# Linear attention in a two-block language-model kernel: keys moved into the exponent, a new order of the score levels, and the read-out and norm by halves

## The reference

```python
def step(state, inp):
    qb, kb, vb, gb = inp
    cum = jnp.cumsum(gb, axis=2)
    o_inter = jnp.einsum('bhtk,bhkv->bhtv', qb * jnp.exp(cum), state)
    rel = cum[:, :, :, None, :] - cum[:, :, None, :, :]
    decay = jnp.exp(jnp.where(causal, rel, -jnp.inf))
    scores = jnp.einsum('bhtk,bhsk,bhtsk->bhts', qb, kb, decay)
    o_intra = jnp.einsum('bhts,bhsv->bhtv', scores, vb)
...
forget = lower_bound + (1.0 - lower_bound) * jax.nn.sigmoid(f.astype(F32))
logf = jnp.log(forget)
k = 1.0 - forget
...
o = rms_norm(o, out_norm) * jax.nn.silu(heads(g.astype(F32)))
return o.reshape(b_, s_, D_MODEL).astype(x.dtype) @ w_out
```

## Time and profile before

| | |
|---|---|
| median of 3 runs | 1805.54 us (1802.91 to 1806.9) |
| the profiled execution | 1802.63 us, span 1800.2 us |
| PE / DVE / ACT / POOL busy | 1717.4 / 1275.4 / 995.2 / 188.5 us |
| linear attention, W0 to the first `down` | 1174.1 to 1274.1 us of the span |

### The profile page before, as it was taken

One profiled execution on the slowest core, in us unless ns is written; L12 is line 12 of the kernel. 1 busy time (PEld: TensorE's weight loads), 2 busy tenths in 40 slices (PEclk: granted clock), 3 DMA queues, 4 the chain that ended last, 5 costly groups with the idle time before them and its releaser, 6 DMA issues.

```text
span 1800.2 us, 35518 instructions
## 1 busy us (share of the span) xinstructions
PE 1717.4 (95%) x11627; PEld 1576.6 (88%) x11627; DVE 1275.4 (71%) x2201; ACT 995.2 (55%) x1476; POOL 188.5 (10%) x108
## 2 busy tenths in 40 slices
PE   7999999999999999999999999999899998799998
PEld 6998879999989999978888887978699998689997
DVE  5866664589997777767777777798666665566665
ACT  6653445675756666644545555654455455564554
POOL 0022300234220000000000000075000000100000
PEclk9999999999999999999999999999899999899999
DMA  5542255577765555567787776442255554045553
GB/s 186 164 151 72 81 178 198 164 210 216 207 214 175 175 175 175 178 217 243 238 280 238 243 239 225 155 138 94 82 188 188 186 185 136 34 141 187 185 185 107
DMA packets 114412, 316.67 MB, mean 176 GB/s; under 512 B 12752, under 2 KB 45904, under 8 KB 113840
## 3 DMA queue, kind: packets, MB, share of 16 engines
q1 hardware_dynamic: 113504, 311.88, 53.7%
q0 software_dynamic: 848, 4.00, 0.6%
HBM read 296.95 MB, written 18.87 MB: 175 GB/s over the span
## 4 chain that ended last, share of the span: by engine, by line
PE 83%; DVE 11%; ACT 3%; issue 2%; DMA 0%; POOL 0%; ACTq 0%; DVEq 0%; SPq 0%; POOLq 0%
PE bank L259 14%; PE bank L260 14%; PE bank L261 14%; PE bank L301 10%; PE bank L302 10%; PE bank L303 10%; PE bank L1288 3%; DVE wlo L243 2%; DVE arena L1860 1%; PE bank L1691 1%; PE bank L996 1%; ACT whi L235 1%; DVE arena L1876 1%; DVE arena L1408 1%; DVE h L452 1%
## 5 line engine op out<-in xcount | busy, mean ns | idle before, releaser
L243 DVE TENSOR_TENSOR wlo<-raw,whi 128x1024 fp32r<-128x1024 f32 x502 | 637.5, 1273 | 218.6 <-ACT whi L235 206.5
L259 PE MATMUL bank<-xhi,whi 128*128 128x256 f32 (+1 forms) x2424 | 707.0, 292 | 14.6 <-DVE wlo L243 7.8
L261 PE MATMUL bank<-xhi,wlo 128*128 128x256 f32 (+1 forms) x2424 | 690.3, 285 | 0.0
L260 PE MATMUL bank<-xlo,whi 128*128 128x256 f32 (+1 forms) x2424 | 690.1, 285 | 0.0
L235 ACT ACTIVATE whi<-raw 128x1024 fp32r<-128x1024 f32 x524 | 550.9, 1053 | 110.3 <-PE bank L303 58.6
L259 PEld LDWEIGHTS bank<-xhi,whi 128*128 128x128 f32 x2424 | 466.8, 193 | 23.5 <-issue 13.4
L260 PEld LDWEIGHTS bank<-xlo,whi 128*128 128x128 f32 x2424 | 467.5, 193 | 1.7
L261 PEld LDWEIGHTS bank<-xhi,wlo 128*128 128x128 f32 x2424 | 466.5, 192 | 0.0
L301 PE MATMUL bank<-whi,yhi 128*128 128x512 f32 x816 | 320.9, 393 | 8.8 <-DVE ylo L585 4.4
L302 PE MATMUL bank<-wlo,yhi 128*128 128x512 f32 x816 | 319.9, 392 | 0.0
L303 PE MATMUL bank<-whi,ylo 128*128 128x512 f32 x816 | 319.3, 391 | 0.0
(11 more groups left out here) (288 smaller groups left out, 1570.6 us busy)
## 6 DMA issues: line engine op xcount, KB each, us to landing
raw<-in_stream SPq DMA_DIRECT2D x524, 512.0 KB, 3.5
act_spill<-h SPq DMA_DIRECT2D x128, 128.0 KB, 3.0
h<-act_spill SPq DMA_DIRECT2D x128, 128.0 KB, 3.3
h<-in_x SPq DMA_DIRECT2D x1, 1024.0 KB, 5.1
arena<-in_keys POOLq DMA_DIRECT2D x1, 1024.0 KB, 6.5
h_spill<-h SPq DMA_DIRECT2D x1, 1024.0 KB, 7.7
arena<-h_spill POOLq DMA_DIRECT2D x1, 1024.0 KB, 5.9
arena<-in_g_final POOLq DMA_DIRECT2D x1, 512.0 KB, 8.0
```

The source lines that it names most:

```text
L243: nc.vector.tensor_tensor(wlo[:, q * 1024:(q + 1) * 1024], raw[:, q * 1024:(q + 1) * 1024], whi[:, q * 1024:(q + 1) * 1024].bitcast(F32), ...
L259: nc.tensor.matmul(bank[b][:, 0:T], whi[:, w], xhi[:, x], start=k == 0, stop=False)
L260: nc.tensor.matmul(bank[b][:, 0:T], whi[:, w], xlo[:, x], start=False, stop=False)
L261: last = nc.tensor.matmul(bank[b][:, 0:T], wlo[:, w], xhi[:, x], start=False, stop=k == KT - 1)
```

## The change

Keys go into the exponent: ACT takes the logarithm of the keys (`CKN`, one more 128x2048 activation after the forget gates' logarithm), POOL subtracts it from `CUM` head by head (eight 128x256 instructions), and the key side of a level is then one exponential. `k_side` is gone from DVE and POOL; `differences` becomes two 128x1024 instructions instead of one of 128x2048. The order of the levels on PE is 8, 0, 1, ..., 7, and which slabs follow each level stands in `AFTER`: two slabs and one in turn. Level matmuls wait for the banks of the level before one by one, and W8 for the copied value banks one by one. The read-out, squares, sums, roots and gating go by halves (heads 0 to 3, then 4 to 7); the norm and the gate are one DVE instruction per head and token tile; the norm's gain is a per-partition scalar `ONC` (one more transpose, of `ONR`), applied when the result is split, straight from PSUM, so that the copy to SBUF and POOL's multiplication are gone. The second half's eight transposes stand between D2 and D3.

```diff
+        LEVEL_ORDER = (8, 0, 1, 2, 3, 4, 5, 6, 7)
+        AFTER = {8: (2,), 0: (3, 4), 1: (5,), 2: (6, 7), 3: (8,), 4: (9, 10), 5: (11,), 6: (12, 13), 7: (14, 15)}
...
+            pe.wait_ge(s("onr_in"), 16)
+            nc.tensor.transpose(bank[7][:, 0:P], ONR, ident[:, :]).then_inc(s("onr_tr"), 1)
             pe.wait_ge(up_evac, U_HG + 16 + 2)
...
+            wide(0)
+            wide(1)
+            pe.wait_ge(s("q_silu"), 1)
+            pe.wait_ge(s("onc"), 1)
+            for x in LEVEL_ORDER:
+                level(x)
+                for k in AFTER[x]:
+                    wide(k)
             pe.wait_ge(s("level_out"), 4 * 9)
...
+            read_out(0)
+            read_out(1)
             pe.wait_ge(s("g_out"), 4)
...
+            turned_out(0)
+            down(pe, N_HGO, D_HGO, 0, 0, 4, first=True)
+            down(pe, N_HGO + 1, D_HGO + 1, 0, 0, 4)
+            down(pe, N_HGO + 2, D_HGO + 2, 0, 0, 4)
+            pe.wait_ge(y_lo, D_HGO + 4)
+            turned_out(1)
...
+                if j == 2:
+                    nc.scalar.activation(CKN, KK, ACT.Ln, bias=LEAST).then_inc(s("logk"), 1)
...
+            level_exp(0)
+            split(0)
+            level_exp(1)
+            for k in (1, 2, 3):
+                split(k)
+            for x in range(2, 8):
+                level_exp(x)
+                for k in AFTER[x - 2]:
+                    split(k + 1)
...
+            split(0)
+            q_side(0)
+            split(1)
+            split(2)
             take(8)
...
+            q_side(1)
+            split(3)
+            for x in range(8):
+                take(x)
+                for k in AFTER[x]:
+                    if k < 15:
+                        split(k + 1)
+                if x + 2 < 8:
+                    q_side(x + 2)
...
+            sums(0)
+            sums(1)
+            gated(0)
+            gated(1)
+            y(0)
...
+            for hd in range(HG_H):
+                q = slice(hd * SEQ, (hd + 1) * SEQ)
+                pool.wait_ge(s("cum"), hd + 1)
+                nc.gpsimd.tensor_tensor(CKN[:, q], CUM[:, q], CKN[:, q], ALU.subtract).then_inc(s("ckn"), 1)
+            pool.wait_ge(s("ckn"), 8)
```

More of the change, by code:

```diff
@@ L1701, in pe_hgrn @@
-            level(8)
-            pe.wait_ge(s("level_out"), 4 * 9)
[L1703 to L1713, removed]
@@ L1714, in pe_hgrn @@
-            pe.wait_ge(s("g_out"), 4)
[L1715 to L1722, removed]
@@ L1723, in pe_hgrn, with read_out @@
-            down_pe(pe, N_HGO, D_HGO, 8)
+            wide(0)
[6 more added lines that the diff above has]
+                    wide(k)
+            pe.wait_ge(s("level_out"), 4 * 9)
+            def read_out(half):
+                for tt in range(TT):
+                    for hd in range(4 * half, 4 * half + 4):
+                        o = bank[4 + 2 * tt + half][:, (hd % 4) * P:(hd % 4 + 1) * P]
+                        v = lambda c: VT[:, c * D + hd * P:c * D + (hd + 1) * P]
+                        if tt == 0:
+                            last = nc.tensor.matmul(o, PP[:, hd * SEQ:hd * SEQ + P], v(0), start=True, stop=True)
+                        else:
+                            nc.tensor.matmul(o, CR[:, hd * P:(hd + 1) * P], v(0), start=True, stop=False)
+                            last = nc.tensor.matmul(o, PP[:, hd * SEQ + P:(hd + 1) * SEQ], v(1),
+                                                    start=False, stop=True)
+                    last.then_inc(s("o_mm"), 1)
@@ new lines, in turned_out @@
+            def turned_out(half):
+                pe.wait_ge(s("o_gated"), 8 * half + 8)
+                for j in range(4):
+                    for tt in range(TT):
+                        c = tt * D + (4 * half + j) * P
+                        last = nc.tensor.transpose(bank[j][:, half * SEQ + tt * P:half * SEQ + (tt + 1) * P],
+                                                   OO[:, c:c + P], ident[:, :])
+                    last.then_inc(s("o_tr"), 1)
+            read_out(0)
+            read_out(1)
@@ L1725, in act_hgrn, with halves @@
+        def halves(ap, half):
+            return ap.rearrange("p (t a h) -> p a t h", t=TT, a=2)[:, half]
         def act_hgrn(act, chain):
@@ new lines, in act_hgrn @@
+            split(0)
[6 more added lines that the diff above has]
+                    split(k + 1)
+                    if k == 7:
+                        act.wait_ge(slabs_done, N_HG + 16 + 8 + RING)
+                        for b in range(4):
+                            nc.scalar.activation(VT[:, b * 512:(b + 1) * 512], bank[b][:, :], ACT.Copy)\
+                                .then_inc(s("v_out"), 1)
@@ L1772, in act_hgrn @@
+            for k in (12, 13, 14):
+                split(k + 1)
+            nc.scalar.activation(tiny[:, 29:30], V("one"), ACT.Silu)
             act.wait_ge(slabs_done, N_HG + 32 + RING)
-            for b in O_ORDER:
+            for b in (0, 2, 1, 3):
                 nc.scalar.activation(GS[:, b * 512:(b + 1) * 512], bank[b][:, :], ACT.Silu).then_inc(s("g_out"), 1)
-            nc.scalar.activation(tiny[:, 28:29], V("one"), ACT.Sqrt)
[L1777 to L1780, removed]
@@ L1797, in dve_hgrn @@
+            squares(0)
+            nc.scalar.activation(tiny[:, 28:29], V("one"), ACT.Sqrt)
+            squares(1)
+            roots(0)
+            roots(1)
+            y(0)
+            for j in range(7):
+                y(j + 1)
+                split_hi(act, N_HGO + j + AHEAD, 0, 0, 4)
         def dve_hgrn(dve, chain):
@@ new lines, in gated @@
+            def gated(half):
+                dve.wait_ge(s("o_rt"), half + 1)
+                chain.link(nc.vector.reciprocal(halves(ORS, half), halves(ORT, half)))
+                for tt in range(TT):
+                    b = 2 * tt + half
+                    if half == 0:
+                        dve.wait_ge(s("g_out"), tt + 1)
+                    else:
+                        dve.wait_ge(s("g_out"), 4)
+                    for hd in range(4):
+                        q = slice(b * 512 + hd * P, b * 512 + (hd + 1) * P)
+                        nc.vector.scalar_tensor_tensor(out=OO[:, q], in0=bank[4 + b][:, hd * P:(hd + 1) * P],
+                                                       scalar=ORS[:, 4 * b + hd:4 * b + hd + 1], in1=GS[:, q],
+                                                       op0=ALU.mult, op1=ALU.mult).then_inc(s("o_gated"), 1)
@@ L1921, in pool_hgrn @@
+            y(0)
+            for j in range(7):
+                y(j + 1)
+                split_lo(dve, N_HGO + j + AHEAD, 0, 0, 4)
         def pool_hgrn(pool, chain):
```

180 lines of the change are left out of this document (84 added, 96 removed).

## The result

The changed kernel takes 1813.31 us (median of 5 runs, 1811.25 to 1813.89), the kernel before beside it 1804.92 us (5 runs, 1802.68 to 1806.9): ratio 1.0041, 95% interval 1.0027 to 1.0056. It is slower by 8.4 us; 1809.2 was forecast. The profiled execution took 1811.25 us, with a span of 1809.6.

A forecast was written before the change was run, and what follows sets the result against it. PE, busy 95% of the span, was taken as the bound, so only its waits could be gained. Levels +5.7 us and tail -2.0 gave +3.7, or 1809.2 us on the median; range 1806.5 to 1813.5.

The forecast's parts named there:

- The start: From the last `up` slab to level 0: PE waits 5.3 us, in two or three pieces; level 0 starts at 1191.6.
- rival A: Start of the levels: scans pass POOL, so level 0 starts 4.2 us sooner; 1805.0 us, within 0.2%; chance 0.20.
- 22.6 us in all: DVE and POOL's shared budget until difference 1 is done: scans 4.8, splits 4.6, subtractions 5.6, halves 7.6 us.
- The next chain: From level 0's end to level 2: 17.0 us against 12.2 us of cover, so PE waits 4.8 us.
- The rest of the levels: From level 2 on: PE has 50.3 us of work plus small waits, ending W15 at 1263.8; levels cost 5.7 us more.
- I add 1.4 us in all, and 1.7 for one fall of the clock: From level 2 on: allowance for chains of 11.5 to 14 us against 12.2, and for slower clock behind longer waits.
- The tail: From the read-out to D0: 12.8 us, 3.1 sooner; 1.1 us of transposes return between D2 and D3; gain 2.0.
- The rest of the kernel is the same: Outside the changed linear attention: no difference in time was charged.
- B: Levels: cheap start and chains that fit, level 2 at 1202.7; 5.7 us faster, 1799.8 us; chance 0.20.
- C: POOL's difference halves cost 2.37 us each, adding 12 us; 1817.5 us; chance 0.12.
- in ACT's waits: Before the scans: the keys' logarithm, 1.9 us on ACT, hides while ACT waits for `up` slabs.
- the first to ask goes first: Throughout the levels: POOL and DVE's SBUF instructions share one time budget, served in order of asking.

The follow-up runs named there:

- spaced: Changed kernel with slabs respread, two after nearly every level and none behind level 7: median 1808.42 us, ratio to before 1.0023.
- third_buffer: Changed kernel with three QK buffers instead of two, so a difference waits for an earlier level's matmuls: 1800.11 us, one execution.
- tail_only: Kernel before with only the new read-out, norm, gating and result split; old keys and level order: median 1804.56 us, ratio 0.9999.
- no_sub: Changed kernel without POOL's eight subtractions of the keys' logarithm, keys left out of all levels but level 8: median 1804.01 us, ratio 0.9997.
- levels_only: Changed kernel with the old tail: only keys in the exponent, new level order and places, banks freed singly: median 1813.19 us, ratio 1.0040.
- sub_on_dve: Changed kernel with the keys' logarithm subtracted by DVE in two 128x1024 instructions behind the first split after the scans: 1804.29 us, one execution.
- three_edits: Changed kernel with three QK buffers, the keys' logarithm subtracted on DVE, and level 8's take directly behind slab 0's split: median 1796.46 us, ratio 0.9945.
- replanned: Changed kernel with the subtraction on DVE and a new written order on all three engines, two buffers: median 1796.91 us, ratio 0.9952.

## Why the prediction was nearly right

The sign, the places and the mechanisms hold; the sizes less so. Forecast for the stage +3.7 us, measured +4.6, and that it came so near is in part luck, since errors of 2.8 and 1.4 us stand against one of 6.1. The time lies 0.2 us inside the upper end of my range (1806.5 to 1813.5); the difference of 8.4 us lies outside my +1 to +8.

*The start, forecast 5.3 us of waits.* Measured 1.13 + 0.37 + 1.40 = 2.9. Scans do take turns with POOL's subtractions (7.16 us), so rival A's premise fell; the last `up` slab waited 1.13 us. But difference 1 ended at 1185.41 us, 60.8 after the stage began, where my sum gave 1185.1 - 1122.05 = 63.0. The term "22.6 us in all" was too large: from 1165.76 to 1185.41 it took 19.7. Scans and subtractions together took 9.2 us, so a subtraction added about 0.55 us where I took 0.7, and the rest of splits and halves took 10.5 for 12.2, in part because the first split (from 1172.84) ran beside the last subtractions. Level 2 began 85.6 us into the stage, 2.8 sooner than the sum says (1210.4 - 1122.05 = 88.4).

*The next chain, forecast 17.0 us and a wait of 4.8.* Measured from level 0's end (1193.6) 16.6 and 4.79. `spaced` shows the cover to be the cause, `third_buffer` the chain.

*The rest of the levels, the step that failed.* The term that was mis-sized is "I add 1.4 us in all, and 1.7 for one fall of the clock": the waits are 1.93 + 2.20 = 4.1 us, and two levels were slowed, by 2.7 and 1.7 us. I had taken the later chains as 11.5 to 14 us against 12.2 of cover and charged almost nothing for it. The longer wait also cost more clock than the one that I copied from the earlier trace rows. From level 2 to the read-out PE took 58.1 us, where I had 53.4. In `third_buffer`, where nothing waits on this stretch, it took 48.9 us (1209.54 to 1258.42), where my sum has 50.3. So waits and clock cost 9.2 us for my 3.1, and 1.4 of these 6.1 us were hidden by slabs and levels priced too high, 2.8 by the overestimate at the start. (The 3.62 us that I read as a level in the earlier trace rows are rows of 30 matmuls; a level there has 32, as the row of 5.46 us says, and not 16.)

*The tail, forecast 12.8 us to D0 and -2.0 in all.* 12.2 us to D0. In all -3.7 + 0.8 = -2.9 us in the changed kernel, and -2.7 in `tail_only`.

*"The rest of the kernel is the same."* True of the code, not of the time: 2.3 us in the windowed attention, in both profiles, at a lower granted clock. If the unprofiled executions behave alike, which no run shows, that makes with the stage's 4.6 us 6.9 of the 8.4 between the medians; the remaining 1.5 lie within the interval (4.9 to 10.1 us), and the starts alone scatter by more. The distance of 4.1 us from my 1809.2 would then be 0.9 from the stage and 2.3 from there; what is left is not more than this scatter.

*The rivals.* A and B needed a cheap start. `no_sub` gave one, and levels 2, 4 and 5 still waited: B's chains don't fit in this order. C's price was not met: alone a half takes 1.93 us, key half or not; the means over the levels, 2.46 us for a query half and 2.93 for a key half, hold the waits for DVE. That the keys' logarithm hides "in ACT's waits" was not wholly so: the scans began 41.1 us into the stage, as in `no_sub` and `levels_only`, which have it too, and 40.5 before and in `tail_only`, which don't.

The Trainium skill (SBUF — State Buffer, "Who interferes with whom") has a DVE instruction with two SBUF inputs contend with a GpSimd one that reads SBUF. For scans this case now shows it (7.16 us beside POOL, 4.75 in `sub_on_dve` with POOL idle). It shows also that the four takes of level 8, which read PSUM, took 2.65 us beside POOL's halves in `three_edits`, against 2.55 with POOL idle.

## What to carry to other kernels

When work leaves engines that are busy but not the bound, ask what the bound waits for: here a chain through four engines from one level to the next but one. With less work the chain into level 2 was no shorter (16.6 us; before, level 2 began 16.4 us after level 0 had ended, at 1183.1, and did not wait), new work ahead of it delayed it, and a new order of PE's work took cover from it. One more buffer (8.8 us) or a better written order (14.2 us with the subtraction moved) was worth more, in the stage, than the arithmetic that the change saved. And compare stages between two marks in the trace before explaining a few us between medians: outside the stage identical code moved by up to 8.8 us.

## What was not expected of the hardware

Who goes next between DVE and POOL depends on more than who asks first, so the prediction's "the first to ask goes first" is not enough. Scans and 128x256 subtractions took turns, 7.16 us for eight. Yet five 128x1024 instructions of DVE went past a POOL half that had begun while a sixth ran; the half took 8.49 us, and in `three_edits` and `replanned` 8.48 again. Each time DVE ran without a pause. What decides it stays open.
